# Hybrid decoder step on one core: the final norm's row spread by TensorE, and one pair's down weights issued earlier

## The reference

```
h = rmsnorm(x, norm_mix); parts = split(h @ w_in)
merged = sigmoid(gate_a) * (window_attention(parts) @ w_proj_attn) + sigmoid(gate_b) * (gla(parts) @ w_proj_gla)
x = x + merged @ w_out
h2 = rmsnorm(x, norm_ffn)
g* = argmax softmax(h2 @ w_rg + b_rg)                 # one of 4 groups
top-2 of the 8 experts of g*; w1, w2 from a softmax times p(g*)
x = x + sum over the two experts: w * ((silu(h2 @ w_gate) * (h2 @ w_up)) @ w_down)
y = rmsnorm(x, norm_final)                             # x * rsqrt(mean(x*x) + eps) * norm_final
```

## Time and profile before

| | us |
|---|---|
| median of 3 runs | 801.12 |
| lowest, highest | 799.43, 801.98 |
| the profiled execution | 798.9 |
| its span, first to last instruction | 796.9 |

### The profile page before, as it was taken

The page is one execution under the profiler, slowest core; times in us unless marked ns, Lnnn a source line. Parts: engine busy times, 40 slices in busy tenths (PEclk is TensorE's granted clock), DMA queues, the critical chain, the costliest instruction groups (busy, mean ns, idle before and its releaser), DMA issues.

```text
span 796.9 us, 12373 instructions
## 1 busy us (share of the span) xinstructions
PE 712.0 (89%) x5116; PEld 531.9 (67%) x5116; DVE 340.5 (43%) x629; ACT 244.8 (31%) x494; POOL 82.6 (10%) x136
## 2 busy tenths in 40 slices
PE   4999999999999999999999999979999977777730
PEld 3888997778999998878999977854444422322210
DVE  6652359564555337435345532741323211111128
ACT  6234374644454343334222232411111100110013
POOL 2404000000000100000000010221213121111100
PEclk9999999999999999999999999999999999999975
DMA  8731111113231622514134199889999999999945
GB/s 314 229 107 62 54 53 53 54 53 108 61 98 54 264 82 107 211 53 114 45 88 121 58 316 388 303 324 362 419 417 418 418 418 417 419 418 419 409 169 203
DMA packets 82632, 173.01 MB, mean 217 GB/s; under 512 B 8065, under 2 KB 42209, under 8 KB 82561
## 3 DMA queue, kind: packets, MB, share of 16 engines
q1 hardware_dynamic: 72736, 148.51, 50.4%
q0 software_dynamic: 9840, 23.72, 8.0%
HBM read 163.25 MB, written 18.74 MB: 228 GB/s over the span
## 4 chain that ended last, share of the span: by engine, by line
PE 66%; SPq 16%; DVE 7%; DMA 5%; ACT 3%; issue 2%; POOLq 0%; ACTq 0%; DVEq 0%
PE bank L755 44%; SPq L564 12%; PE bank L1214 6%; SPq L570 3%; PE bank L1230 3%; DMA expert_down<-in_w_exp_down 2%; DVE w_split L1584 2%; ACT w_split L1268 1%; PE bank L775 1%; PE bank L1185 1%; PE bank L1040 1%; DMA token_out<-token_out_scratch 1%; PE bank L1046 1%; DVE s_state L1888 1%; DMA x_rows<-in_x_prompt 1%
## 5 line engine op out<-in xcount | busy, mean ns | idle before, releaser
L755 PE MATMUL bank<-hT_split,w_split 128*128 128x272 f32 x1152 | 154.1, 292 | 0.0
L755 PEld LDWEIGHTS bank<-hT_split,w_split 128*128 128x128 f32 x1152 | 147.4, 188 | 2.1 <-issue 0.9
L1214 PE MATMUL bank<-expert_gate_up,gatheredT 128*64 128x512 f32 x512 | 116.7, 603 | 21.5 <-DMA expert_gate_up<-in_w_exp_up 20.6
L755 PE MATMUL bank<-w_split,hT_split 128*128 128x512 f32 (+1 forms) x576 | 130.1, 380 | 0.7 <-DVE w_split L1584 0.7
L755 PEld LDWEIGHTS bank<-w_split,hT_split 128*128 128x128 f32 x576 | 100.1, 188 | 23.1 <-issue 3.3
L1584 DVE TENSOR_TENSOR w_split<-w_raw,w_split 128x2048 fp32r<-128x2048 f32 (+1 forms) x35 | 75.9, 2168 | 83.4 <-ACT w_split L1268 83.4
L1214 PEld LDWEIGHTS bank<-expert_gate_up,gatheredT 128*64 128x64 f32 x512 | 39.7, 138 | 95.6 <-issue 64.1
L1268 ACT ACTIVATE w_split<-w_raw 128x2048 fp32r<-128x2048 f32 (+1 forms) x35 | 63.4, 1812 | 42.1 <-PE bank L755 17.6
L1230 PE MATMUL bank<-expert_down,expert_actT 128*64 128x512 f32 x256 | 58.5, 598 | 12.6 <-DMA expert_down<-in_w_exp_down 7.6
L2146 DVE TENSOR_TENSOR expert_act<-expert_silu,bank 128x256 f32<-128x256 f32 x16 | 6.7, 421 | 121.6 <-ACT expert_silu L1539 121.6
L755 PE MATMUL bank<-gla_outT_split,w_split 128*128 128x272 f32 x384 | 49.4, 288 | 0.0
(11 more groups left out here) (367 smaller groups left out, 828.9 us busy)
## 6 DMA issues: line engine op xcount, KB each, us to landing
expert_gate_up<-in_w_exp_gate SPq DMA_DIRECT2D x64, 512.0 KB, 14.9
expert_gate_up<-in_w_exp_up SPq DMA_DIRECT2D x64, 512.0 KB, 15.1
expert_down<-in_w_exp_down SPq DMA_DIRECT2D x32, 1024.0 KB, 17.1
w_raw<-in_w_in SPq DMA_DIRECT2D x15, 1024.0 KB, 5.5
w_raw<-in_w_in SPq DMA_DIRECT2D x16, 512.0 KB, 4.7
s_state<-in_state_gla POOLq DMA_DIRECT2D x4, 1024.0 KB, 10.3
out_sample_gla_state<-s_state POOLq DMA_DIRECT2D x4, 1024.0 KB, 6.1
w_raw<-in_w_proj_gla SPq DMA_DIRECT2D x8, 512.0 KB, 4.3
```

The lines of the kernel that those rows point to most:

```text
L755: ins = mm(out, stat(x, k), mov(y, k), start=first and n == 0 and m == 0, stop=last and n == len(ks) - 1 and m == 2)
L1214: ins = mm(P[2 + u][64 * half:64 * half + 64, :].rearrange("p (m n) -> p m n", m=2), XT[0][:, k, 64 * half:64 * half + 64], WGU[gb][:, k / ...
```

## The change

It has two parts. `norm_final` is loaded as one row of 4 KB into partition 0 of `NFIN`. DVE writes a row of 128 ones (`ONEROW`, one partition) ahead of L2046. PE, once `norm_final` has landed, multiplies the ones by the row, 512 columns at a time, into banks 2 and 3, ahead of its last clock keepers, which become 5 instead of 6. ACT copies both banks into `NFIN`, ahead of the first turned rows. The final norm waits for ACT instead of for the two loads, and the waits on `scattered` lose their extra 16; those of the first scatters go.

SP issues the down weights of pair 2 when POOL has issued the first two gathers (`gathers_issued`), not when both have landed. SP's wait for the second table goes as well.

```diff
@@ memory
+    ONEROW = at("ones_row", [1, 128], F, W0 + 32256)
@@ SP
             load_down(1, pair(1), (1,))
-            sp.wait_ge(rows_ready, 2)
-            for u in range(2):
-                sp.wait_ge(gathered[u], 16)
+            sp.wait_ge(gathers_issued, 1)
             load_down(2, pair(2))
...
-            sp.wait_ge(scattered[0], 16 * turns + 16)
-            sp.wait_ge(scattered[1], 16 * turns + 16)
+            sp.wait_ge(scattered[0], 16 * turns)
+            sp.wait_ge(scattered[1], 16 * turns)
@@ POOL
-            for u in range(2):
-                c = slice(D // 2 * u, D // 2 * u + D // 2)
-                pool.dma_start(NFIN[:, c], a["norm_final"].partition_broadcast(128)[:, c]).then_inc(scattered[u], 16)
+            pool.dma_start(NFIN[0:1, :], a["norm_final"].unsqueeze(0)).then_inc(nfin_in, 16)
...
             for u in range(2):
                 gather(u, IDXG[:, u:u + 1])
+            pool.sem_inc(gathers_issued, 1)
             pool.wait_ge(rows_ready, 2)
...
-                pool.wait_ge(scattered[u], 16 * i + 16)
+                if not isinstance(i, int) or i:
+                    pool.wait_ge(scattered[u], 16 * i)
@@ PE
             pe.wait_ge(lg_out, NB)
-            keep_clock(6)
+            pe.wait_ge(nfin_in, 16)
+            for c in range(2):
+                ins = mm(P[2 + c][:], ONEROW[:], NFIN[0:1, 512 * c:512 * c + 512], start=True, stop=True)
+            ins.then_inc(nfin_mm, 1)
+            keep_clock(5)
             pe.wait_ge(gathered[0], 16)
             turn_rows(0)
@@ ACT
             A(DUMMY[:], EPSC[:], ACT.Silu)
+            act.wait_ge(nfin_mm, 1)
+            A(NFIN[:, 0:512], P[2][:], ACT.Copy)
+            A(NFIN[:, 512:D], P[3][:], ACT.Copy).then_inc(nfin_out, 1)
...
-                act.wait_ge(scattered[1 - u], 16 * i + 16 + 16 * u)
+                if not isinstance(i, int) or i + u:
+                    act.wait_ge(scattered[1 - u], 16 * i + 16 * u)
@@ DVE
+            V.memset(ONEROW[:], 1.0)
             link(V.memset(IF1[:], float(NOTOK)))
...
-                dve.wait_ge(scattered[1 - u], 16 * i + 16 + 16 * u)
+                if not isinstance(i, int) or i + u:
+                    dve.wait_ge(scattered[1 - u], 16 * i + 16 * u)
...
-            for u in range(2):
-                dve.wait_ge(scattered[u], 16)
+            dve.wait_ge(nfin_out, 1)
```

More of the change, by code:

```diff
@@ L480, in decoder_step @@
         pool_passed = sem("pool_passed")
+        gathers_issued = sem("gathers_issued")
+        nfin_in, nfin_mm, nfin_out = sem("nfin_in"), sem("nfin_mm"), sem("nfin_out")
         out_rows, x3_ready = sem("out_rows"), sem("x3_ready")
```

## The result

The changed kernel takes 802.32 us (median of 13 runs, 798.55 to 803.35). The kernel before, run beside it, takes 799.90 (13 runs, 797.52 to 801.98). The ratio is 1.0025, 95% interval 1.0014 to 1.0036: about 2.0 us slower by the ratio, 2.4 by the medians. That is within the 0.3% named ahead, but on the other side than forecast (798.8), and 0.2 us outside the range given (796.6 to 802.1). The forecast started from the 801.12 of three runs; from the 799.90 of thirteen its terms give 797.6, so the miss is larger than the two times beside each other show.

What follows compares the result with a forecast made beforehand. The weight stream starting with pair 3's loads was taken to set the end. From the profiled 798.9 us, -0.4 (gather) and -1.9 (clock) gave 796.6; off the 801.12 median, 798.8 us, range 796.6 to 802.1.

Steps and rivals of the forecast that it cites:

- What bounds the kernel: From pair 3's first weight load on, an unbroken weight stream sets the end, which moves only as that stream starts earlier.
- SP's part: Down weights of pair 2 issued at 528.9 instead of 532.88: worth 0, bounds 0 and -0.5 us.
- Rival C: Early down weights slow gather 0 to 6.9 us, the chain starts 0.95 later, the clock dips: 802.1 us; chance 0.12.
- The sign that I had named: At the first two gathers: the forecast is wrong if they land later than 532.8.
- The gather term: Gather 0, with a lighter stream ahead and down weights arriving at its end: -0.4 us, bounds -1.0 to +1.0.
- The clock term: PE's shorter idle before the first row turn keeps its clock up through gate-up: -1.9 us, bounds -1.94 and 0.
- The clock stays: Assumption that PE's clock holds 1.00 in 535 to 540, its idle stretches being about 1.1 and 0.9 us.
- The rest at 0: Norm row landing, POOL's load, DVE's memset, PE's products, ACT's copies, dropped waits and final norm: each taken as 0.

Runs made afterwards that it cites:

- e1_sp_only: The kernel before with SP's part alone, down weights of pair 2 issued on `gathers_issued`, norm row loaded spread as before: 801.87 us, ratio 1.0024 to before.
- e5_norm_end: The kernel before with the norm row loaded as one row, its products and ACT's copies behind the last pair of experts: 798.57 us, ratio 0.9989 to before.
- e6_keep12: The kernel before with 12 clock keepers instead of 6 ahead of the first row turn, nothing else: 798.32 us, ratio 0.9980 to before.
- e2_norm_only: The changed kernel with SP's part undone, SP waiting for the second table and both gathers as before: 797.72 us, ratio 0.9977 to before.
- e3_issue_done: The changed kernel with `gathers_issued` raised by a small POOL memset behind both gathers instead of a bare semaphore increment: 797.18 us, ratio 0.9974 to before.
- e4_one_row: The kernel before with its 6 keepers replaced by two unread one-row f32 products of 512 columns and 5 keepers: 798.48 us, ratio 0.9988 to before.
- e13_early_norm_end: The changed kernel with one-row products and ACT's copies moved behind the last pair, and 6 keepers: 802.73 us, ratio 1.0042 to before.
- e14_early_keep16: The changed kernel with 16 keepers instead of 5 behind the one-row products: 802.05 us, ratio 1.0039 to before.
- e9_six_one_row: The kernel before with its 6 keepers replaced by six unread one-row f32 products of 512 columns: 802.53 us, ratio 1.0034 to before.
- e8_full_rows: The kernel before with its 6 keepers replaced by two unread f32 products of 128 rows, 512 columns, and 5 keepers: 797.65 us, ratio 0.9975 to before.
- e10_six_full_rows: The kernel before with its 6 keepers replaced by six unread f32 products of 128 rows and 512 columns: 798.66 us, ratio 0.9985 to before.

## Why the prediction was wrong, and where it was right

**What bounds the kernel: right.** "The end moves only by as much as this stream starts earlier" holds in all 18 executions (256.3 to 257.5 us from pair 3's first load to the end), in the losing direction too.

**SP's part: right that it is worth 0, wrong on when it issues.** The step that failed is "it goes on when POOL has issued the second gather, at 527.87 + 1.03 = 528.9". I read the increment behind the gathers as POOL's engine reaching it. Measured: 527.05 in the changed kernel, 527.48 in `e1_sp_only`, in both about 0.35 us after POOL's first gather began. A signal that does wait for the engine gives 529.47, near the 528.9 I had, and then the kernel gains what I had forecast: 797.18 us against 799.91 before, 2.7 us for 2.3.

**Rival C was the mechanism as far as it says that the early load delays the gathers, and its size was too small.** I had given it 0.12, with the condition "if the down weights are in the engines before about 530". "Against it" I had put that gather 0 is issued 2.6 us before them; it was 0.36. C's price had the gather at 6.9 us, the median of the stream's gathers, as its upper bound. Measured 7.8 in `e1_sp_only`, 9.1 in the changed kernel. That bound was no bound, although those 16 gathers had more than 2 MB queued at their side: they land within 7.3 us, and the two of the changed kernel did not. So sharing the engines with a full queue, which is how C was priced, is not all of it; the gathers also began late, with no packet of POOL's queue from 1.3 to 4.4 us after the issue. The Trainium skill, page "DMA: Bandwidth & Descriptors", section "Queues, rings and completion order", has the queues take turns on each engine. The runs agree in direction, as 5.96 us became 7.8 to 9.1, but this alone does not say why the first packet was late. The sign that I had named came true: both gathers landed later than 532.8, at 535.7 and 537.5.

**The gather term, -0.4: of the wrong sign here.** In the changed kernel's profile it is +3.15, the term of the sum that was missed most. Without the early load the -0.4 is borne out in size, not proved: `e5_norm_end`, which has the light norm row and not the early weights, gives 5.58 us against 5.96, one execution each and no more than the scatter of that gather.

**The clock term, -1.9: near in size, not reached, and not by the way forecast.** `e6_keep12` gains 1.69 us on the gate-up by bridging the wait alone; at full clock the first half takes 3.69 us (534.58 to 538.27), not the 3.44 of the second. In the changed kernel the clock was down from 530 on, the wait was 3.67 us, not 1.1, since the gather came late, and the turn and the gate-up ran into the low clock: +0.81 and +0.65 instead of -1.9. "The clock stays" did not hold even where the gather was in time: in `e2_norm_only` and `e3_issue_done` it fell during the products and keepers, and their gate-up of 7.09 us is owed to its being back in time, which the prediction did not foresee. But I also priced the one-row products by their columns alone, as cover for PE. Their duration was right (1.96 us for 1.9), and six of them show that as cover for the clock they are worth less than products of 128 rows. In the time of the change itself this is not seen: `e2_norm_only` gains 0.23%, more than `e4_one_row`'s 0.12%, in line with a shorter wait and a lighter queue together, though the intervals overlap. That gain is lost once the gather is late (`e13_early_norm_end`, 802.73), so the two parts don't add.

**The rest at 0: right.** The norm row took 9.5 us to land (by 525.4; I had put its latest time at 526.1), and PE came to the products at 526.71 with no wait; the 518 worked out from the page "DMA: Bandwidth & Descriptors" of the Trainium skill, section "Anatomy of one DMA", an estimate by its 2.0 us for a load, was much too early. ACT's copies stood at 528.70 to 529.8, long before the turned rows. Nothing in the final norm shows a wait for them.

**What stays open.** Why an early load keeps the gathers' first packets back; why the changed kernel's own gathers took 9.1 and 9.2 us and those of the others with the same load 7.8 to 8.4, one profiled execution each; how the delay grows with the bytes; and whether the early down weights, rightly signalled, gain about 1 us beside a held clock.

## What to carry to other kernels

A bare semaphore increment in POOL's list said only that the list had been read that far, not that the engine had done the work ahead of it; to hold other loads back until a gather is really under way, let an instruction of that engine behind it give the signal (here a memset), or wait for the landing. Before moving a load forward ask what small, latency-bound transfer it will share the engines with: here 2 MB moved forward brought nothing and cost its neighbour 2 to 3 us. Where an engine's wait for such a transfer lets the clock fall ahead of long work, a few full-size products in the wait are the cheaper gain (six more keepers, 0.9980); too many, or a fall of the clock under them, make PE late for the transfer (`e14_early_keep16`, 10.61 us).

## What the runs showed of the hardware that was not expected

- POOL's semaphore increment, placed behind two indirect DMAs, let SP issue 0.3 to 0.4 us after the first had begun, 1.2 to 1.3 us before the second began and 2.2 to 2.3 us before it was through (changed kernel, `e1_sp_only`). A memset in its place gave the signal at 529.45, at the end of the second.
- The first two gathers of 128 rows of 4 KB, which land in 4.7 to 7.1 us without such loads, took 7.8 to 9.2 with 1 to 2 MB of loads queued at their side, or ahead of them, and POOL's queue moved no packet from 1.3 to 4.4 us after the first one's issue. The later ones, in the full stream of before, took 6.1 to 7.3.
- TensorE's granted clock fell to 0.50 within a stretch of one-row products in which the engine was busy 1.00 of each microsecond (`e9_six_one_row`, 529 to 531).
- Two idle stretches of nearly the same length went both ways: 1.42 and 0.90 us in `e8_full_rows` kept the clock at 1.00, 1.44 and 0.90 in `e10_six_full_rows` did not (0.50 in 535 to 537).
- A load of 4 KB took 9.5 us to land behind a queue of weights, nearly as long as the two of 256 KB that it replaced (10.6).
